# Hybrid decoder layer on 8 cores: mLSTM normalizer on GpSimd, norm statistics two tiles ahead, weights piece by piece, last output tile in groups of 512 columns

## What is computed

```
h = rms_norm(x, norm);  proj = h @ w_in
# A: mLSTM, 4 heads of 256
qk = silu(causal_depthwise_conv(m_qk, conv_w, conv_b));  mq, mk = split(qk)
hm = mlstm_chunkwise(mq, mk, m_v, ig, lf)     # h = num / max(|den|, 1), stabilised
hm = rms_norm(hm, mh_norm) * sigmoid(m_o) * silu(m_z)
# B: latent attention, 8 heads
q = rms_norm(a_cq, cq_norm) @ w_uq;  kv = rms_norm(a_ckv, ckv_norm) @ w_ukv
ha = causal_attention(rope(q), rope(k), v) * silu(a_z)
# C: attention into 256 memory tokens
mkv = rms_norm(mem, mem_norm) @ w_mem_kv
hc = softmax(c_q k / 16) v * silu(c_z)
merged = g_m * (hm @ w_br_m) + g_a * (ha @ w_br_a) + g_c * (hc @ w_br_c)
out = rms_norm(x + merged @ w_out, final_norm)
```

## Time and profile before

| | |
|---|---|
| median of 3 runs | 2828.43 us (2826.03 to 3314.26) |
| the profiled execution's own time | 2809.95 us |
| its span, first to last instruction, slowest core | 2808.7 us |
| spans of the 8 cores | 2790.4 to 2808.7 us |
| PE busy | 2703.5 us (96%) |
| DVE, ACT, POOL busy | 1097.6, 924.2, 533.7 us |
| mean granted TensorE clock of the 8 cores | 0.990 to 0.993 |

### The profile page before, as it was taken

How to read it: one execution, slowest core, us unless ns; L and a number is a source line. 1 busy time by engine, 2 the same in 40 slices (tenths; PEclk the granted TensorE clock), 3 DMA queues, 4 the chain that set the end, 5 groups by cost and what they waited for, 6 DMA issues and landing times.

```text
span 2808.7 us, 41624 instructions; the slowest of 8 cores (2790.4 to 2808.7 us)
## 1 busy us (share of the span) xinstructions
PE 2703.5 (96%) x14037; PEld 1331.3 (47%) x14037; DVE 1097.6 (39%) x2011; ACT 924.2 (33%) x1808; POOL 533.7 (19%) x636
## 2 busy tenths in 40 slices
PE   6989999999999999989889999999999999999998
PEld 3544444674547544445445544444444444444443
DVE  4635466448584467355553411111111111110433
...
GB/s 229 144 87 155 219 62 102 98 84 102 80 62 132 83 57 60 114 126 165 98 104 137 190 79 76 79 76 78 73 168 76 110 74 76 79 79 127 195 206 77
DMA packets 140817, 310.26 MB, mean 110 GB/s; under 512 B 14337, under 2 KB 72513, under 8 KB 133441
## 3 DMA queue, kind: packets, MB, share of 16 engines
...
...
## 4 chain that ended last, share of the span: by engine, by line
PE 89%; DMA 4%; ACT 3%; DVE 2%; issue 2%; SPq 0%; DVEq 0%; POOL 0%; ACTq 0%; POOLq 0%
PE bk L289 87%; DMA xo<-x 1%; PE bk L488 1%; DMA kr<-KRT 1%; DMA mv<-MV 1%; DMA cz<-CZ 1%; ACT junk L293 0%; DMA QNT<-ob 0%; ACT e L293 0%; DVE xb L309 0%; DMA mb<-BH 0%; SPq L134 0%; ACT L293 0%; DVE e L309 0%; ACT DT L293 0%
## 5 line engine op out<-in xcount | busy, mean ns | idle before, releaser
L289 PE MATMUL bk<-hT,wg 128*128 128x512 bf16 x3072 | 682.0, 380 | 0.0
L289 PE MATMUL bk<-w,hT 128*128 128x512 bf16 (+1 forms) x3072 | 604.6, 347 | 18.8 <-DVE e L309 4.1
L289 PE MATMUL bk<-hT,w 128*128 128x512 bf16 x2112 | 492.5, 381 | 3.4 <-ACT e L297 2.0
L289 PEld LDWEIGHTS bk<-hT,wg 128*128 128x128 bf16 x3072 | 300.9, 98 | 361.3 <-issue 1.6
L289 PEld LDWEIGHTS bk<-w,hT 128*128 128x128 bf16 x3072 | 298.6, 98 | 269.3 <-issue 33.7
L293 ACT ACTIVATE sh<-bk 128x512 f32<-128x512 f32 x184 | 109.9, 597 | 849.1 <-PE bk L289 849.1
L289 PE MATMUL bk<-hb,wb 128*128 128x512 bf16 x1536 | 346.7, 379 | 0.0
L289 PEld LDWEIGHTS bk<-hT,w 128*128 128x128 bf16 x2112 | 205.8, 98 | 234.6 <-issue 9.2
L309 DVE SCALAR_TENSOR_TENSOR tm<-sh,bk 128x512 f32<-128x512 f32 x124 | 85.3, 688 | 559.2 <-PE bk L289 559.2
L289 PEld LDWEIGHTS bk<-hb,wb 128*128 128x128 bf16 x1536 | 150.3, 98 | 181.0
L302 DVE TENSOR_TENSOR den<-den,Pa 128x512 f32<-128x512 f32 (+3 forms) x288 | 180.3, 626 | 119.3 <-ACT Pa L293 108.2
...
## 6 DMA issues: line engine op xcount, KB each, us to landing
wg<-wGB POOLq DMA_DIRECT2D x96, 512.0 KB, 5.8
...
```

The lines of the kernel that those rows point to most:

```text
L289: fw.op("pe", lambda e: e.matmul(bk[o] if not isinstance(o, bass.AP) else o, lhsT=lhsT, rhs=rhs, start=start, stop=stop), reads=reads, wri ...
```

## The change

Six parts, none of which changes what is computed:

1. `rsqrt` and the three operations ahead of it in `P2n` move from DVE to POOL. `rsqrt` now has 13 operations, since the fused multiply-add is two and the shift is folded into one; with the three that is 16 small ones for a chunk.
2. The add of `DT` moves to POOL as two adds (mask, then A broadcast), emitted at the start of chunk c for c+2 (`P1d`); ACT then takes one Exp over all heads. `mv` gets a third buffer and is loaded one chunk earlier. Tiles are laid out in another order, and the yields inside a chunk are redistributed (their sum stays 4.04).
3. Weight pieces go to a list; once `uq` is done, one is issued for each 5 us of ideal dense matmul time, and `w_get` issues what is left.
4. In `p0_gen` one `step` holds the square of tile i+2 and the square of the latest c result with one Ln and one Exp for both. A c result is turned one step later. The gain copies are all on DVE, the first five tiles are written in two halves and copied to `hT` by DVE alone, and the first weight load waits for the gain row, not for tile 0.
5. In the "cq" section all 16 units run alike; the memory tiles come at units 3 to 7; the three sines wait until the second head of `p1_gen`, and the last c results are finished inside the first.
6. The last output tile is squared, multiplied by `gfin` and at last scaled in four groups of 512 columns, with ACT and DVE in turn for the scaling and ACT's and SP's queues for the stores.

Core of the diff:

```
         def rsqrt(y, x, t, r):
-            V(lambda e: e.tensor_scalar(out=ti, in0=xi, scalar1=1, scalar2=None, op0=ALU.logical_shift_right))
-            V(lambda e: e.tensor_scalar(out=yi, in0=ti, scalar1=-1.0, scalar2=-550241825.0, op0=ALU.mult, op1=ALU.add))
+            ts("pool", yi, xi, -0.5, -550241825.0, ALU.mult, ALU.add, [r], [r])
             for c in (3.0, 12.0, 768.0):
-                V(lambda e: e.tensor_tensor(out=t, in0=y, in1=y, op=ALU.mult))
-                V(lambda e: e.tensor_tensor(out=t, in0=t, in1=x, op=ALU.mult))
-                V(lambda e: e.scalar_tensor_tensor(out=y, in0=t, scalar=-c, in1=y, op0=ALU.add, op1=ALU.mult))
+                tt("pool", t, y, y, ALU.mult, [r], [r])
+                tt("pool", t, t, x, ALU.mult, [r], [r])
+                ts("pool", t, t, -c, None, ALU.add, None, [r], [r])
+                tt("pool", y, t, y, ALU.mult, [r], [r])
...
-                fw.dma("pool", t[:, c], flat[:, c], writes=[t.rs[j]])
+                wpend.append((name, lambda c=c, j=j: fw.dma("pool", t[:, c], flat[:, c], writes=[t.rs[j]])))
+            pace(0)
...
+        def pace(d):
+            paced["d"] += d
+            while wpend and (not paced["on"] or paced["d"] >= 5.0):
+                wpend.pop(0)[1]()
+                paced["d"] = 0.0
...
+            def step(x=None, c=None):
+                if x in cur:
+                    act(junk[:], cur[x][:], AF.Square, [cur[x].r], [junk.r, r], scale=1.0 / math.sqrt(D), accum_out=sj[:, 4 * k:4 * k + 1])
...
+                if c:
+                    which, t_, bk, r_bk = c
+                    act(jc[:], bk[:, 0:512], AF.Square, [r_bk], [jc.r] if cs else [jc.r, r], accs=[r] if cs else [], scale=1.0 / math.sqrt(512.0), accum_out=sj[:, 4 * k + 1:4 * k + 2])
+                    cs.append(1)
+                if cs:
+                    rstd(sj[:, 4 * k + 2 + cs[0]:4 * k + 3 + cs[-1]], sj[:, 4 * k + cs[0]:4 * k + 1 + cs[-1]], r)
...
-            fw.wait_res("pool", cur[0].r)
+            fw.wait_res("pool", grow.r)
...
+            for t_ in range(NT):
+                if t_ in (5, 7):
+                    trans(16 if t_ == 5 else 17)
                 settle()
+                if t_ in (3, 5):
+                    step(x=16 + t_ // 5)
+                    write(16 + t_ // 5)
                 yield from c_unit(1, t_, w)
...
+            while not P.get("sing"):
+                yield
             act(a_[:], ang[:], AF.Sin, [ang.r], [a_.r])
...
+            def P1d(c):
+                B2, DT = B2s[c % 3], DTs[c % 2]
+                Av = At[:].rearrange("p (h t) -> p h t", h=4)[:, :, c:c + 1].to_broadcast([128, 4, 128])
+                tt("pool", DT[:], B2[:], Mneg[:].unsqueeze(1).to_broadcast([128, 4, 128]), ALU.add, [B2.r, Mneg.r], [DT.r])
+                tt("pool", DT[:], DT[:], Av, ALU.add, [DT.r, At.r], [DT.r])
...
-                tt("dve", DT[:], B2[:], Mneg[:].unsqueeze(1).to_broadcast([128, 4, 128]), ALU.add, [B2.r, Mneg.r], [DT.r])
                 act(EB[:], B2[:], AF.Exp, [B2.r], [EB.r])
-                for h in range(4):
-                    act(DT[:, h, :], DT[:, h, :], AF.Exp, [DT.r, At.r], [DT.r], bias=At[:, h * 16 + c:h * 16 + c + 1], scale=1.0)
+                act(DT[:], DT[:], AF.Exp, [DT.r], [DT.r])
...
             for c in range(16):
+                if c + 2 < 16:
+                    P1d(c + 2)
                 P2(c, 0)
...
-                loads_v(c + 2)
+                loads_v(c + 3)
...
+            def olast(t):
+                for n4 in range(4):
+                    ounit(t, n4)
+                    osq(t, n4)
+                    tt("dve", yt[:, n], xt[:, n], gfin[:, n], ALU.mult, [xt.rs[n4], gfin.r], [yt.rs[n4]])
...
+                for n4 in range(4):
+                    if n4 % 2:
+                        ts("dve", yt[:, n], yt[:, n], sto[:, c + 5:c + 6], None, ALU.mult, None, [yt.rs[n4], r_s], [yt.rs[n4]])
+                    else:
+                        act(yt[:, n], yt[:, n], AF.Copy, [yt.rs[n4], r_s], [yt.rs[n4]], scale=sto[:, c + 5:c + 6])
+                    fw.dma("sp" if n4 % 2 else "act", out_d[t * 128:(t + 1) * 128, n], yt[:, n], reads=[yt.rs[n4]])
```

More of the change, by code:

```diff
@@ L2 @@
 import contextlib
+import itertools
 import numpy as np
@@ L541, in p0_gen @@
                 mm(bk, r_bk, (slice(None), slice(0, 512)), onesf[0:1, :], grow[0:1, n * 512:(n + 1) * 512], True, True, [grow.r, RM])
-                copy("act" if n % 2 else "dve", gx[:, n * 512:(n + 1) * 512], bk[:, 0:512], [r_bk], [], accs=[gx.r])
+                copy("dve", gx[:, n * 512:(n + 1) * 512], bk[:, 0:512], [r_bk], [], accs=[gx.r])
+            mem.release(grow)
+            t16 = Ring(tiles("c16_", 6, [128, 512], BF16, top=True))
             bks = [DB.next() for _ in range(4)]
-            for i in range(4):
-                stats(i)
+            act(sj[:, 188:189], onesf[:, 0:1], AF.Ln, [RM], [sj.rs[47]])
+            step(x=0)
+            for i in range(5):
+                step(x=i + 1)
                 write(i)
@@ L699, in p1_gen @@
                                        lambda bk, r_bk: part(o, cols, bk, r_bk, tb == 0), q=4)
+                    if hh == 0 and tb in (1, 3):
+                        P["settle"]()
+                if hh == 1:
+                    P["p0_end"]()
+                    P["sing"] = True
+                    for _ in P["tg"]:
+                        pass
+                    trig_spread()
+                    cosT, sinT = P["cos"], P["sin"]
+                    t1s = Ring(tiles("ro", 4, [128, 512], F32))
                 fw.dma("sp", KNT_d[hh * 128:(hh + 1) * 128, :], o[:], reads=[o.r], accs=[dr("KNT", hh)])
@@ L1521, in d_gen @@
                 ofin(t)
-            for t in range(4, NT):
+            for t in range(4, NT - 1):
                 for n4 in range(4):
@@ L1526, in d_gen @@
                 ofin(t)
+            yield from olast(NT - 1)
         def dense_all():
@@ L1567, in build @@
             st["d"] += v
+            pace(v)
             while st["s"] < st["ratio"] * st["d"]:
```

224 lines of the change are left out of this document (114 added, 110 removed).

## The result

The changed kernel takes 0.9705 of the time of the kernel before, 95% interval 0.9664 to 0.9747: 0.9705 of 2828.43 is 2745 us, where 2775 was forecast. Its shown runs are 2743.47 to 3072.91 (median 2770.1 of four); the ratio leaves out executions in which a whole die ran slower, on both sides. The profiled executions take 2744.32 and 2809.95, a difference of 65.6 us where the sum said 53.

A forecast was written before the change was run, and what follows sets the result against it. PE was taken as nearly full for 2304 us, with gains only where it waits. Start 5, "cq" section 15, mLSTM 30, weight pieces 0 and tail 3 sum to 53 us: 2828.43 to 2775, range 2752 to 2812.

The forecast's parts named there:

- About 24 of the 36.5 us of waits to go: mLSTM: PE's idle 36.5 us would shrink by about 24; with two thirds of the clock's 9.2, gain 30 us.
- The median of the runs shown is 18.5 us above that execution: Whole kernel: the 53 us gain was taken from the 2828.43 median instead of the profiled 2809.95, giving 2775.
- The start: First 58.4 us: earlier square and halved xb let tile 4's unit run near 53 us; gain 5 us.
- The "cq" section: 112 to 190 us: moved sines and later turns end the memory tile's wait, others and clock loss; gain 15 us.
- The weight pieces: Weight loads issued piece by piece: gain 0 us elsewhere (-3 to 3), beyond the mv wait.
- The POOL terms: mLSTM: small POOL operations at 0.36 us, two adds of 1.2 each, POOL's work 14.8 us a chunk.
- The tail: After the last add: output tile in four groups with smaller stores, 10.1 us to about 7; gain 3 us.
- POOL becomes the bound: mLSTM: at 0.6 us a small operation POOL needs 18.6 us a chunk; total about 2802; chance 0.11.
- The waits are of the chain: mLSTM: PE keeps waiting for some ACT copy, half the gain (15 us) goes; 2790 us; chance 0.18.
- More goes than forecast: mLSTM waits and clock loss go but for a few, 42 us, and 18 at the start; 2763 us; chance 0.2.
- signs of being wrong: mLSTM: no POOL idle left before hr; PE waits for qe or DT's Exp for POOL; or waits only change names.
- 0.68 us with POOL idle beside it: mLSTM: DVE's DT add was read as 0.68 us beside an idle POOL, against 0.94 in the mean.

The follow-up runs named there:

- the table of the two moves: Changed kernel (mLSTM 263.2 us) with the normalizer back on DVE: 282.1; with DT's add on DVE and four Exps on ACT: 264.5; with both: 301.6.
- the added operations: Changed kernel (mLSTM 263.2 us) with more small POOL operations per chunk, between rsqrt and hr: four more 276.0 us, eight more 299.1 us (ratio 0.9908).

## Why the prediction was wrong

**The range** (2752 to 2812) missed by 7 us, in two steps; either of them alone would have left the time inside it.

*"About 24 of the 36.5 us of waits to go (all of `Cf` and `mv`, 12.7; two thirds of the ACT waits ...) and two thirds of the clock's"*. This is the term that was mis-sized: 30 us, measured 40.7 (median of cores) to 44.8 (slowest). Nearly all waits went, not two thirds: 36.5 became 3 to 8. I took ACT's waits for a cause of their own and cut them by a third; the table of the two moves and the step back from each wait show that they hung on DVE. The clock gave somewhat more than its 6 us: the mean matmul took 167.5 ns (268.51 / 1603) and takes 162.5 (252.08 / 1551), 5 ns x 1580 = 8 us. Of the 40.7 some 2 us are matmuls that only moved behind the stretch.

*"The median of the runs shown is 18.5 us above that execution; I take the same 53 from it"*. The 18.5 us were a thing of their own, which I passed over: a clock of 0.81 behind the old start, which no profile with the new start shows. With the terms as measured and the old clock kept, the forecast would have been 2828 - 66 = 2762, inside the range.

**Point by point.** *The start*, 5 forecast: the unit of tile 4 begins at 51.02 (forecast 53; 58.37 before), 7.4, of which 6.1 are left where the "cq" section begins. *The "cq" section*, 15: 77.4 - 61.5 = 15.9 on the slowest cores, right in size, but of its reasons "the sines" was wrong: with them back the section is 61.6 us long in the median of cores, without 60.9, and PE does not wait for the memory tile. *The weight pieces*, 0: right, since three `mv` buffers cover the bursts. *The POOL terms*: pitch 0.378 for 0.36; the two adds 1.28 and 1.05 for 1.2 each; a POOL chunk of 16.45 - 0.7 = 15.7 for 14.8. The terms that I had come to 14.7 (16 x 0.378 = 6.05, then 2.33, 2.06, 1.90 and 2.35 of `qe`); left out were POOL's products into `e` (8.7 us, 0.54 a chunk) and the issue of weight pieces (7.1 us, 0.44 a chunk), which makes 15.7. *The tail*, 3: 2.7. Here are the last add, the first and the last scaling and the last issue:

```profile
2735.92 0.69 DVE L310 SCALAR_TENSOR_TENSOR xo<-bk,xo 128x512 f32<-128x512 f32 x1 [1.68 <-PE bk L290]
...
2738.20 0.72 ACT L294 ACTIVATE xo<-xo,sto 128x512 f32<-128x512 f32 x1
...
2739.43 0.72 ACT L294 ACTIVATE xo<-xo,sto 128x512 f32<-128x512 f32 x1 [0.50 <-ACT xo L294]
2740.22 0.34 ACTq L135 DMA_DIRECT2D out<-xo  x1
```

Where the earlier trace rows has 10.1 us from the last add to the end, it is 7.4 now, and the last 256 KB store takes 3.1 (2743.3 - 2740.22) for the 2.4 that I guessed.

**The rivals.** "POOL becomes the bound" fell, but by 0.7 us a chunk: at a pitch of 0.42 instead of 0.378 it would have begun to count. "The waits are of the chain" fell: with the two bursts gone PE waits for hardly any copy. "More goes than forecast" is what happened (42 for the mLSTM; measured 40.7 to 44.8). It was given 0.2, and its time, 2763, still lacked the clock; its terms as written, 42, 18 and 3, give 2765, and 18 for the start is less than the forecast's own 20.

**The signs.** Of the signs of being wrong two came: POOL has next to no idle time left before `hr` (2.1 us), and the Exp of `DT` waits 5.8 us for POOL. Both are also what a POOL with 0.7 us of room in a chunk looks like, so they could not tell the case from its rival; only the added operations did. **A reading:** "0.68 us with POOL idle beside it" is not so. The add at 1361.54 meets the last 0.1 us of `hr` and runs 0.4 us into `hmt`, which then takes 2.30 us; two other adds that begin 0.3 us behind `hmt` take 2.33 and raise the mean to 0.94. The rule that is cited there from "SBUF — State Buffer" of the Trainium skill, section "Who interferes with whom", agrees with these rows.

**Not forecast**: 4.0 us are given back between the mLSTM and the first output tile. 2.3 of them are the last chunk's `hmt`, which comes out of POOL's longer chain; the rest is the 13 matmuls that now stand behind the mLSTM's end (on the six cores with whole records PE's busy time there grew by 1.8 us and its idle time by 1.9).

## What to carry to other kernels

A wait on an in-order engine belongs to whatever stands ahead of the producer on its list: before sizing what a burst costs, follow each small wait one step further back, and count those that lead to it whole. Two fixes for one burst are not worth their sum; undo each with the other in place and without it. And where some executions of the kernel before lie apart from its profiled one, look for a core that ran a stretch at a lower clock, since the change may take that away or leave it; the per-core clocks of the unprofiled executions are enough to see it.

## What the chip showed beside

A small dependent POOL operation (128 x 4) is 0.20 to 0.24 us busy and 0.378 apart from the next, where DVE's stand (1359.45 - 1355.94) / 13 = 0.27 apart: a factor of 1.4. The mask's add of 512 columns took POOL 1.28 us and DVE 0.68, a factor of 1.9. The add of A, one value for each 128 columns, took POOL 1.05; that of the mask, 128 columns repeated for the four heads, took 1.28, about as much as an add of two full operands (1.264). A DVE add of two SBUF operands that begins just behind a large POOL product of two takes 2.33 us instead of 0.68; begun before it, it lengthens the product by 0.24. And a granted clock of 0.81 held for 150 us (1300 to 1450) on two neighbouring cores, with PE busy throughout, while core 0 of the same die had 0.94 to 0.99.
